# Input projection as seven products of halves in a hybrid pooling and gated DeltaNet block, side work of the delta branch on other engines

## The reference

```python
xn = rmsnorm(h, norm_w)                      # h: 16 meta tokens + 512 tokens, 2048 channels, float32
proj = xn @ w_in                             # 2048 x 14368
u_pool, z_pool, q, k, v, z_dn, b, a, gate_pool, gate_dn = split(proj)
y_pool = causal_multiscale_pool(u_pool) * silu(z_pool)
y_dn = gated_deltanet_branch(q, k, v, z_dn, b, a, ...)     # 16 heads of 128, conv of 4 taps, decay, beta
merged = sigmoid(gate_pool) * (y_pool @ w_pool_out) + sigmoid(gate_dn) * (y_dn @ w_dn_out)
out = rmsnorm((h + merged @ w_o)[16:], final_norm_w)
```

## Time and profile before

| | |
|---|---|
| runs, us | 1962.31, 1962.41, 1963.60 (median 1962.41) |
| profiled execution: its span, us | 1960.8 (the profile has no second time for it; the median of the runs is 1.6 above) |
| busy: TensorE, VectorE, ScalarE, GpSimd | 99%, 47%, 37%, 4% |
| granted TensorE clock, mean | 0.997 |
| HBM read and written, MB | 199.65, 25.30 |

### The profile page before, as it was taken

One profiled execution on the slowest core, in us unless ns is written; L12 is line 12 of the kernel. 1 busy time (PEld: TensorE's weight loads), 2 busy tenths in 40 slices (PEclk: granted clock), 3 DMA queues, 4 the chain that ended last, 5 costly groups with the idle time before them and its releaser, 6 DMA issues.

```text
span 1960.8 us, 35753 instructions
## 1 busy us (share of the span) xinstructions
PE 1931.4 (99%) x13729; PEld 1724.3 (88%) x13729; DVE 921.4 (47%) x2315; ACT 726.0 (37%) x2136; POOL 78.3 (4%) x105
## 2 busy tenths in 40 slices
PE   5999999999999999999999999999999999999998
PEld 5888899999999999999999988888888888888886
DVE  6333343656556466555646654322224444335332
ACT  5422223435353443535345353323234322224232
POOL 4000000000000000000000000000000000000000
PEclk8999999999999999999999999999999999999999
DMA  6133342433333242333334144333443534347302
GB/s 222 59 103 102 102 134 88 119 95 86 95 120 90 87 124 69 96 111 100 91 107 123 44 131 127 119 107 128 134 162 134 186 118 139 118 139 279 108 22 86
DMA packets 221302, 225.73 MB, mean 115 GB/s; under 512 B 33665, under 2 KB 197978, under 8 KB 220522
## 3 DMA queue, kind: packets, MB, share of 16 engines
q1 hardware_dynamic: 158898, 180.17, 28.1%
q10 hardware_dynamic: 55944, 22.63, 4.6%
q0 software_dynamic: 6336, 21.08, 3.4%
HBM read 199.65 MB, written 25.30 MB: 115 GB/s over the span
## 4 chain that ended last, share of the span: by engine, by line
PE 97%; ACT 1%; DVE 1%; issue 0%; POOL 0%; DMA 0%; ACTq 0%; SPq 0%; DVEq 0%
PE pj L530 82%; PE pg L530 10%; PE pt L530 3%; PE pt L679 1%; PE pg L781 0%; POOL xl L1696 0%; DVE fst L1233 0%; ACT xsquare L908 0%; DMA xt<-in_meta_tokens 0%; PE pj L574 0%; DVE xl L1239 0%; ACT wh L868 0%; DVE xt L1246 0%; ACT L1041 0%; ACT L1070 0%
## 5 line engine op out<-in xcount | busy, mean ns | idle before, releaser
L530 PE MATMUL pj<-xh,wh 128*128 128x512 f32 (+3 forms) x2688 | 735.1, 328 | 3.2 <-DVE wl L1208 3.1
L530 PE MATMUL pj<-xh,wl 128*128 128x512 f32 (+3 forms) x2688 | 712.4, 319 | 0.0
L530 PE MATMUL pj<-xl,wh 128*128 128x512 f32 (+3 forms) x2688 | 712.3, 319 | 0.0
L1208 DVE TENSOR_TENSOR wl<-raw,wh 128x256 fp32r<-128x256 f32 x896 | 344.2, 421 | 603.0 <-ACT wh L868 601.5
L530 PEld LDWEIGHTS pj<-xh,wh 128*128 128x128 f32 x2688 | 446.9, 189 | 43.2 <-DVE wl L1208 3.4
L530 PEld LDWEIGHTS pj<-xh,wl 128*128 128x128 f32 x2688 | 448.4, 188 | 35.9
L530 PEld LDWEIGHTS pj<-xl,wh 128*128 128x128 f32 x2688 | 448.8, 189 | 33.9 <-issue 1.0
L868 ACT ACTIVATE wh<-raw 128x256 fp32r<-128x256 f32 x896 | 307.0, 410 | 64.7 <-issue 45.0
L868 ACT ACTIVATE wh<-rawb 128x256 fp32r<-128x256 f32 (+1 forms) x224 | 85.0, 437 | 217.0 <-PE pj L530 189.8
L530 PE MATMUL pj<-yl,wh 128*128 128x512 f32 x384 | 149.5, 389 | 0.0
L530 PE MATMUL pj<-yh,wl 128*128 128x512 f32 x384 | 149.5, 389 | 0.0
(11 more groups left out here) (243 smaller groups left out, 1784.3 us busy)
## 6 DMA issues: line engine op xcount, KB each, us to landing
raw<-in_w_in SPq DMA_DIRECT2D x112, 1024.0 KB, 6.2
rawb<-in_w_dn_out SPq DMA_DIRECT2D x16, 1024.0 KB, 6.3
rawb<-in_w_o SPq DMA_DIRECT2D x12, 1024.0 KB, 5.3
gates_scratch<-stg ACTq DMA_DIRECT2D x32, 256.0 KB, 2.1
rawb<-in_w_pool_out SPq DMA_DIRECT2D x8, 1024.0 KB, 5.7
gst<-gates_scratch POOLq DMA_DIRECT2D x32, 256.0 KB, 3.1
yraw<-branch_scratch SPq DMA_DIRECT2D x1, 5632.0 KB, 23.1
xt<-in_x SPq DMA_DIRECT2D x4, 1024.0 KB, 6.2
```

What stands on the lines that cost most here:

```text
L530: return pe.matmul(dst, lhs, rhs, start=start, stop=stop)
L1208: tt(wl[:, j, 2 * q:2 * q + 2, :], raw[:, 2 * par + h, 2 * q:2 * q + 2, c * P:(c + 1) * P], wh[:, j, 2 * q:2 * q + 2, :].bitcast(F32), ALU ...
```

## The change

The projection is made by Strassen's scheme (the variant with sums of sums) on halves: the 2048 channels are cut in two, the 256 columns of a block in two, and the 528 tokens in two of 264 (8 meta tokens and 256 tokens each). Seven products of halves replace eight. The token side is made once, in the prologue: `xh[i]`, `xl[i]` for seven operands. On the weight side each block loads four quarters of 128 columns (`raw`, slots RA, RB, RE, RF), and VectorE makes four sums in place (S1 to S4). A product is 8 k tiles in two chunks of 4 (12 matmuls each); a block is 14 chunks (16 in the first, 12 in the last block), because the product that a block could begin with is run in the block before (`NEXT`). Weight buffers are a ring of five slots of 4 k tiles. The matmul writes 264 columns (k, v, u), 260 (q) or 256. Three partial results are copied out of PSUM by ScalarE while the bank goes on accumulating (`snap`), and VectorE makes three of the four output quarters by an addition or subtraction (`c21`, `c22`, `c11`, 256 or 264 elements). The fourth is evacuated as before.

The delta steps keep their arithmetic and their place on TensorE, two hooks (12 matmuls of a half) to a step: 56 steps in four blocks. The forward substitution starts at step W0 = 11 in seven steps of two columns, the assembly of the inverse at step 26, the chunk steps at 32. Moved to ScalarE: the subtraction in the decay (10 small activations instead of two on GpSimd), the first tap of each convolution, SiLU of each convolved half, the copies and negations in the assembly, the last scaling of the output. Moved to GpSimd's queue: all transfers of the two trips through DRAM. New: q, k, v, z of each pair go through a DRAM scratch (`head_d`, eight stores of 264 KB on ScalarE's queue, three loads on SP's queue between the loads of weight quarters), since their buffers in SBUF now hold the token operands. The small projection for beta and decay moves to the third block. The diff, cut to its core:

```diff
+NEXT = 0
+ORDER_FIRST = (1, 2, 7, 6, 4, 5, NEXT, 3)
+ORDER = (7, 6, 4, 2, 5, NEXT, 3)
+ORDER_LAST = (7, 6, 4, 2, 5, 3)
+AHEAD = 4
+RINGS = 5
+HK = KH // 2
...
+SLOT_OF = {1: 0, NEXT: 0, 2: 1, 3: 1, 4: 3, 5: 3, 6: 2, 7: 2}
+RA, RB, RE, RF = range(4)
...
-        raw = lay.tensor("raw", [4, UK, CW])
-        xh = lay.tensor("xh", [KT, TP], F32R)
-        xl = lay.tensor("xl", [KT, TP], F32R)
-        wh = lay.tensor("wh", [4, UK, P], F32R)
-        wl = lay.tensor("wl", [4, UK, P], F32R)
...
+        raw = lay.tensor("raw", [4, KH, P])
+        wh = lay.tensor("wh", [RINGS, HK, P], F32R)
+        wl = lay.tensor("wl", [RINGS, HK, P], F32R)
+        snap = lay.tensor("snap", [4, TH])
...
-        W0 = F0 + 9
-        NSTEP = 3
+        W0 = F0 + 6
+        NSTEP = 2
+        Q0 = W0 + 7
...
+        def ring_free(b, at):
+            if isinstance(b, int) and b == 0:
+                return at - RINGS + 1
+            return base_of(b) + (at - 3 if at < 4 else -4 if at == 4 else at - RINGS + 1)
...
+        def split_targets(b, t):
+            first, last = isinstance(b, int) and b == 0, isinstance(b, int) and b == NCP - 1
+            n = 2 * len(order_of(b))
+            if first:
+                own = [t + AHEAD]
+            else:
+                own = [3, 4] if t == 0 else [t + AHEAD]
+            found = [(b, at) for at in own if at < n]
+            if not last and t > n - AHEAD:
+                found.append((b + 1, t - n + 3))
+            return found
...
+            def load_kq(d):
+                for c in range(2):
+                    sp.wait_ge(head_stored[c], 64 * d + 32)
+                sp.wait_ge(pe_chunk, base_of(CP_PAIR0 + 4 * d + 3))
+                sp.dma_start(kq[:, :, :, :].rearrange("p a h t -> p (a h) t"),
+                             head_d[bass.ds(d, 1), 0:4, :, :].rearrange("d a p t -> p (d a) t")).then_inc(kq_loaded, 16)
+            def load_vch(d):
+                need(sp, y_stored, 16 * d)
+                for c in range(2):
+                    sp.wait_ge(head_stored[c], 64 * d + 48)
+                sp.dma_start(vch, head_d[bass.ds(d, 1), 4:6, :, :].rearrange("d a p t -> p (d a) t")).then_inc(vch_loaded, 16)
+            def load_zst(d):
+                sp.wait_ge(x_mm, 3 * d + 3)
+                for c in range(2):
+                    sp.wait_ge(head_stored[c], 64 * d + 64)
+                sp.dma_start(zst, head_d[bass.ds(d, 1), 6:8, :, 0:SEQ].rearrange("d a p t -> p (d a) t")).then_inc(zst_loaded, 16)
+            def block_loads(b, col, between=None):
+                order, base = order_of(b), base_of(b)
+                if between == "v":
+                    load_vch(between_pair[0])
+                sp.wait_ge(sum_done, summed(b, "S1"))
+                load_raw(RA, col)
+                if between == "kq":
+                    load_kq(between_pair[0])
+                sp.wait_ge(sum_done, summed(b, "S4"))
+                load_raw(RE, col)
+                if between == "z":
+                    load_zst(between_pair[0])
+                sp.wait_ge(lo_done, base + after(order, 5))
+                load_raw(RF, col)
+                sp.wait_ge(lo_done, base + after(order, 3))
+                load_raw(RB, col)
...
+            def block_products(b, par, kind, kind_next, hook):
+                order, base = order_of(b), base_of(b)
+                first = isinstance(b, int) and b == 0
+                for i, what in enumerate(order):
+                    if what == 7:
+                        need(pe, add_done, added(b - 1, "C21"))
+                    elif what == 6:
+                        pe.wait_ge(snap_done, snapped(b, "s1"))
+                    elif what == 4:
+                        pe.wait_ge(snap_done, snapped(b, "s4"))
+                    elif what == 2:
+                        need(pe, add_done, added(b - 1, "C11"))
+                    elif what == 5:
+                        pe.wait_ge(snap_done, snapped(b, "s2"))
+                    elif what == NEXT:
+                        need(pe, last_done, b)
+                    elif what == 3:
+                        pe.wait_ge(add_done, added(b, "C22"))
+                    c0 = c0_of(kind_next if what == NEXT else kind)
+                    bank = bank_a[par] if what in (1, 6, 5, 3) else bank_a[1 - par] if what == NEXT else bank_c if what == 2 else bank_b
+                    opens, closes = what in (1, 2, 7, NEXT), what in (3, 2, 4)
+                    for h in range(2):
+                        chunk = 2 * i + h
+                        slot = ring_slot(b, chunk)
+                        if first and what in (1, 2):
+                            pe.wait_ge(x_lo_pool, chunk + 1)
+                        elif first and what != NEXT:
+                            pe.wait_ge(x_lo, {7: 1, 6: 3, 4: 5, 5: 7, 3: 9}[what] + h)
+                        pe.wait_ge(lo_done, base + chunk + 1)
+                        for k in range(HK):
+                            kt = HK * h + k
+                            for w, xx, one, last in ((wh, xh, True, False), (wh, xl, False, False), (wl, xh, False, True)):
+                                mm = pe.matmul(bank[:, c0:TH], w[:, slot, k, :], xx[what][:, kt, c0:TH],
+                                               start=opens and one and kt == 0, stop=closes and last and kt == KH - 1,
+                                               skip_group_check=True)
+                            if k == HK - 1:
+                                mm.then_inc(pe_chunk, 1)
+                            if k % 2 == 1:
+                                hook(2 * chunk + k // 2)
...
+            def split_hi(of, at):
+                order = order_of(of)
+                what, half = order[at // 2], at % 2
+                need(act, pe_chunk, ring_free(of, at))
+                if half == 0:
+                    if what in (1, 2, 4):
+                        act.wait_ge(raw_loaded[SLOT_OF[what]], 16 * of + 16)
+                    elif what == NEXT:
+                        act.wait_ge(raw_loaded[RA], 16 * of + 32)
+                    else:
+                        act.wait_ge(sum_done, summed(of, {7: "S3", 6: "S2", 5: "S1", 3: "S4"}[what]))
+                copy(wh[:, ring_slot(of, at), :, :], raw[:, SLOT_OF[what], HK * half:HK * (half + 1), :]).then_inc(hi_done, 1)
...
+                for t in range(2 * len(order)):
+                    for of, at in split_targets(b, t):
+                        split_hi(of, at)
+                    c0 = c0_of(kind)
+                    if 1 in order and t == after(order, 1):
+                        act.wait_ge(pe_chunk, base + t)
+                        copy(snap[:, par, c0:TH], bank_a[par][:, c0:TH]).then_inc(snap_done, 1)
+                    if t == after(order, 7):
+                        act.wait_ge(pe_chunk, base + t)
+                        need(act, add_done, added(b - 1, "C22"))
+                        copy(snap[:, 3, c0:TH], bank_b[:, c0:TH]).then_inc(snap_done, 1)
+                    if t == after(order, 6):
+                        act.wait_ge(pe_chunk, base + t)
+                        copy(snap[:, 2, c0:TH], bank_a[par][:, c0:TH]).then_inc(snap_done, 1)
+                    if NEXT in order and t == after(order, NEXT):
+                        c0 = c0_of(kind_next)
+                        act.wait_ge(pe_chunk, base + t)
+                        need(act, add_done, added(b - 1, "C11"))
+                        copy(snap[:, 1 - par, c0:TH], bank_a[1 - par][:, c0:TH]).then_inc(snap_done, 1)
+                    event(t)
...
-                if m == F0 + 2:
-                    wait(mk_ready, 1, 1)
-                    act.dma_start(full_rows(gram_d), slots(mk)).then_inc(mk_stored, 16)
-                    act.dma_start(blocks(gram_d, NBLK - 2, NBLK).rearrange("a j c -> j a c"), tail(mk)).then_inc(mk_stored, 16)
...
+            def s3(b):
+                dve.wait_ge(raw_loaded[RA], 16 * b + 16)
+                dve.wait_ge(raw_loaded[RE], 16 * b + 16)
+                tt(raw[:, RE, :, :], raw[:, RE, :, :], raw[:, RA, :, :], ALU.add).then_inc(sum_done, 1)
+            def s2(b):
+                dve.wait_ge(raw_loaded[RF], 16 * b + 16)
+                dve.wait_ge(sum_done, summed(b, "S3"))
+                dve.wait_ge(lo_done, base_of(b) + after(order_of(b), 7))
+                tt(raw[:, RE, :, :], raw[:, RE, :, :], raw[:, RF, :, :], ALU.add).then_inc(sum_done, 1)
+            def s1(b):
+                dve.wait_ge(sum_done, summed(b, "S2"))
+                dve.wait_ge(lo_done, base_of(b) + after(order_of(b), 4))
+                tt(raw[:, RF, :, :], raw[:, RE, :, :], raw[:, RA, :, :], ALU.subtract).then_inc(sum_done, 1)
+            def s4(b):
+                dve.wait_ge(lo_done, base_of(b) + after(order_of(b), 2))
+                tt(raw[:, RB, :, :], raw[:, RB, :, :], raw[:, RE, :, :], ALU.add).then_inc(sum_done, 1)
...
+                for t in range(2 * len(order)):
+                    if t == (6 if first else 2):
```

(54 more changed lines are left out.)

1168 lines of the change are left out of this document (705 added, 463 removed).

## The result

The changed kernel takes 2068.9 us (median of 4 runs, 2060.5 to 2072.7) against 1962.8 before: a ratio of 1.053, 95% interval 1.051 to 1.056. It is slower by 106 us; the prediction was 1908, faster. The profiled execution has a span of 2071.0 us, 110.2 over that of before.

A forecast was written before the change was run, and what follows sets the result against it. TensorE's instruction stream was taken to bound the kernel: 1960.8 - 139 (halves) + 80 (pair waits) + 5 (prologue) = 1906.8, with the median 1.6 above the span: 1908 us, range 1830 to 1965.

The forecast's parts named there:

- Price of the halves: Projection blocks on TensorE: seven products of halves in place of eight save 139 us, ends 109 and 158.
- Rival D: Projection matmuls do not halve: 256 columns cost 0.1350 us or more, gate blocks get longer, 1990 us and up; chance 0.02.
- VectorE's load: Pairs: VectorE has about 94 to 96 us of work a pair, 90% full instead of 59%.
- So 10 us a pair: Pairs: waits for the gram and the inverse add 10 us in each of 8 pairs, 80 us back.
- hidden unless one of its waits holds a split: ScalarE in a pair period: some 75 of 105 us busy, costing nothing unless a wait there delays a split.
- 7 us of late splits: Blocks k and q: VectorE waits at step 11 for the gram's round trip, so later splits come late, 7 us a pair.
- 3 us for the inverse: Pairs: TensorE waits at step 26 for the inverse's trip through DRAM, 3 us a pair, ends 0 and 7.
- rival C: Slower: round trips on GpSimd's queue set the pair, waits of 17 to 22 us a pair, 1963 to 2005 us; chance 0.12.
- break-even of 16.8 us a pair: Pairs: waits of 134 / 8 = 16.8 us in each would use up the gain.
- Prologue and pool stage: Start and pool blocks: TensorE starts at about 32.5, block 0 needs 29.5 us, net 5 us lost; pool blocks -15.2.
- branch and output stages: nothing: Stages after the projection: the change neither saves nor costs time there.
- The markers: Signs, right: gate halves 9.8 us apart, pair near 115; wrong: pair 106, or 122 up with GpSimd issues over 1.5.

The follow-up runs named there:

- e4: Changed kernel with VectorE's four weight sums on 8 columns instead of 1024, so the summed quarters are left out: 2036.6 us.
- e7: Changed kernel with TensorE multiplying the identity by itself 9, 13 and 18 times ahead of three waits of each pair: 2027.6 us.
- e12: Changed kernel with only the three pair loops written out, on TensorE, ScalarE and VectorE: 2034.7 us.
- e1: Changed kernel with the scaling of the outputs moved back from ScalarE to VectorE: 2047.5 us.
- e6: Changed kernel with only the two DRAM round trips moved back from GpSimd's queue to ScalarE's: 2027.3 us.
- e11: Changed kernel with scaling on VectorE, inverse, transposes and other steps moved, and pair loops written out on three engines: 1942.1 us, 0.990 of the kernel before.

## Why the prediction was wrong

- *Price of the halves, 139 us: right.* A gate block takes 19.88 us where 19.66 was taken; pair 0 saved 8.7 of 10.6. Rival D is out. The work of a pair at full clock is 106.5 to 107.4 us (105.3 forecast).
- *VectorE's load: right, and it was not the point.* Forecast 94 to 96 us a pair, measured 94.4 (660.50 / 7); ScalarE 75 forecast, 78.0 measured. Yet e4 took 16 us a pair off VectorE and the pair fell by 2.6. "90% full" was turned into late splits; what was late were single results, each behind other work in an in-order queue.
- *The step that failed: "So 10 us a pair".* TensorE idles 17.1 us a pair and pays 7.6 to 8.5 more at half clock: with the 1 to 2 us of added work that is the 132.1 measured against 115.3 forecast. Three terms were missing, and of the one that was there the parts were not as forecast.
  - *The clock.* The prediction priced a wait at its length. In the earlier trace rows it is 1.00 because TensorE never idled there. But the trace of the kernel before does show what an idle stretch costs, at the very matmuls of the earlier trace rows: behind the 3.11 us of idle time before them the clock is 0.50 for 3.4 us, and half as many matmuls fit in as in the next 3.4:

```profile
35.80:39.20 3.40, 3.38 (x15) 3.39 (x16) 3.40 (x4) 3.40 (x12) 3.40 (x3) 0.50 0.02 7
39.30:42.70 3.40, 3.40 (x30) 3.40 (x30) 3.37 (x13) 0.43 (x2) 1.57 (x2) 1.00 0.30 76
```

  After the change, from 645.90 to 649.30, behind idle stretches of 1.7 and 2.4 us, matmuls of 260 columns follow each other every 0.216 us at 0.50 granted, and every 0.119 from 649.4 on. The two windows of the kernel after, 18 matmuls and 30 in the same length:

```profile
645.90:649.30 3.40, 3.40 (x18) 3.40 (x17) 3.40 (x7) 1.93 (x10) 0.68 (x1) 0.50 0.89 197
649.40:652.80 3.40, 3.40 (x30) 3.40 (x30) 2.60 (x5) 1.80 (x3) 0.39 (x1) 1.00 0.59 152
```

  Filled waits (e7) gave back 5.7 us a pair.
  - *The turn of the loop*, 5.4 us a pair (e12). The prediction had it nowhere. In the kernel before TensorE's turns were as long and cost nothing, since queued matmuls of 512 columns covered them; ScalarE's and VectorE's were short.
  - *The scaling on ScalarE*, 3.3 us a pair (e1). It was costed by ScalarE's total ("hidden unless one of its waits holds a split"), not by what stands in front of it in the queue.
  - *The round trips.* Forecast as 7 us of late splits and 3 us for the inverse. The 3 came out (22.0 us in seven pairs, 3.1 a pair). Late splits inside the blocks cost 4.2 a pair, and the copies between the transposes of q and k, which the prediction did not name, 3.6: that block q idles 9.5 us a pair, near the 10, is in part luck. The gram was there 28.6 us into the block k shown, 28 forecast, but from an mk that was 2.2 us later (19.9 instead of 17.7) and a trip that was shorter; step 11 was due at 25.4. The prediction has 23.5 for that, where its own terms (16.1, 5.7 and a split of 0.6) add up to 22.4. On GpSimd's queue the trips cost 5.6 us a pair over ScalarE's (e6), for which rival C's 0.12 was too little. Its break-even of 16.8 us a pair was passed by several causes together, which no rival had.
- These terms overlap (a shorter wait also spares clock, a turn is a wait) and are not to be added: together e11 took off 16.2 us a pair.
- *Prologue and pool stage: forecast -15.2, measured +11.9.* The first block took 40.0 us, not 29.5: there are sixteen token-side operations of 1.17 us on VectorE where 12 were counted, and TensorE ran at half clock in three stretches around its stands (to 41.8, from 52.0 to 55.4 and from 58.8 to 65.7). The fourth block lost 5.6 to ScalarE's table functions.
- *Last block: forecast 16.9, measured 27.5.* The sum that frees a bank stood behind the y and weight splits on VectorE: TensorE idled 8.4 us. The prediction had "branch and output stages: nothing" and did not look at the block in front of them.
- *The markers* did tell: gate blocks short, a pair of 122 or more, GpSimd issues of 0.5 to 1.06 us and not 1.5. By the prediction's own text that was C without its mechanism, which is what it turned out to be.
